# A two-layer decoder trunk: the shared expert's gate and up products moved ahead of the first routed expert, in four PSUM banks

## The chip, the cores and the metric

The kernel runs on one core of one Trainium2 chip. The metric is the device time in microseconds of one execution. A core has a matrix engine (TensorE, PE in the rows), VectorE (DVE), ScalarE (ACT), GpSimd (POOL) and SyncE (SP), which here does nothing but issue transfers. Its 16 DMA engines bring data from HBM into the on-chip SBUF; matrix products land in PSUM, which has eight banks of 128 x 512 float32.

## What is computed

Two decoder layers run over 272 tokens (16 learned ones and 256 of input) of width 1024. Layer 0 mixes tokens with RWKV-7, layer 1 with sliding-window attention. After each mixer stands a mixture of 64 small SwiGLU experts with 8 chosen per token, and one shared expert for all tokens:

```
def swiglu(x, wg, wu, wd):
    return (jax.nn.silu(x @ wg) * (x @ wu)) @ wd

def moe_ffn(x2d, router, bias, w_gate, w_up, w_down, sh_gate, sh_up, sh_down):
    scores = jax.nn.sigmoid(x2d.astype(F32) @ router.astype(F32))
    ...                                   # 4 of 8 groups, then 8 of 64 experts per token
    y = lax.map(expert_block, ...)        # swiglu(x2d[tok], w_gate[e], w_up[e], w_down[e]) * gate
    routed = jax.ops.segment_sum(y.reshape(P, D), slot_tok, num_segments=T)
    return swiglu(x2d, sh_gate, sh_up, sh_down) + routed
```

All is float32. An expert's three matrices (1024 x 256, 1024 x 256 and 256 x 1024) are 1 MiB each, so the 64 experts of a layer are 192 MiB that must be read from HBM.

## The kernel before

Every engine has its program written out by hand, and counting semaphores join them. `Steps` gives each named step of a stage a place in a list, and a later engine waits for "step x is done".

**The expert stage.** Experts are worked off in order, one turn each. In turn e TensorE does the gate and up products of expert e (`mm_gate_up`, L782), turns the gathered token rows of expert e+1 (`mm_turn_x`, L770), picks the token indices of expert e+3 (`pe_pick`, L763: three columns wide), turns the hidden values (`mm_turn`, L789) and does the down product of expert e-1 (`mm_down`, L800). VectorE makes the index lists (`dve_mark`, L807, and `dve_index`, L813 to L815) and copies the turned rows (L775); GpSimd gathers token rows by an indirect DMA (L819) and scatters results (L824).

**Weights.** There are 18 slots of 1 MiB in SBUF, six experts' worth: `ORDER` names them by threes (gate, up, down). SyncE issues the loads, strictly in order. The loads of experts 0 to 4 (15 slots) are issued before the stage. Slots 15, 16 and 17, which belong to expert 5, lie in memory that the router and the shared expert use first: slot 15 holds the shared gate weights, slot 16 the shared up weights, slot 17 part of what the shared products read (`mhT` lies in it in part). `plan_experts` says what frees them. From expert 6 on, the gate and up loads of expert e wait for the gate and up products of expert e-6, and its down load for the down product of expert e-6 (`sp_load`):

```
for slot in (15, 16, 17):
    slot_free[slot] = moe_pe[l].at("su1")
```

**The shared expert.** `mm_shared` makes one of four products: gate and up, each in two halves of the hidden width (`sg0`, `sg1`, `su0`, `su1`), in eight steps over the model width, each step two instructions of 128 x 272 in the trace (L1014). Gate halves both go to bank 7 and up halves both to bank 1, so `sg1` waits until ScalarE has taken `sg0`, and `su1` until VectorE has taken `su0`. `sg0` and `su0` run while VectorE ranks the experts; `sg1` and the first half of `su1` come after the picks of experts 0 to 2; the second half of `su1` is in turn 0, behind `mm_turn`. The six down products (`mm_shared_down`, L1024) are in turns 1, 2 and 3, two in each. `keep_busy` (L1005) issues matrix products whose result nobody reads.

Of the kernel before, what the change touches and what calls it, by code (L numbers as in the profile page):

```python
# [123 lines left out]
def hybrid_trunk(nc, I, out):  # L124
    with ExitStack() as ctx:
# [127 lines left out]
        def ln_steps(t, halves=True):  # L253
# [25 lines left out]
        H_ORDER = [(0, 2, 1), (1, 2, 0)]  # L279
        ROW_ORDER = [(0, 1, 0, 2, 1), (1, 0, 1, 2, 0)]  # L280
        moe_pe = [Steps(sem(f"route_pe{l}"), [(f"hT{t}", 1 if t == 2 else 2) for t in H_ORDER[l]]
                        + [("lg", 1), ("sT", 1), ("sg0", 1), ("su0", 1), ("pos", 1), ("sg1", 1), ("su1", 1), ("sd", 6)])
                  for l in range(2)]
        moe_act = [Steps(sem(f"route_act{l}"), [(f"hT{t}", 1) for t in H_ORDER[l]] + [("sig", 1), ("sc", 1), ("sg0", 1), ("sg1", 1)]) for l in range(2)]
        moe_dve = [Steps(sem(f"route_dve{l}"),
                         [(f"{n}{t}", 1) for n, t in zip(("hT", "hT", "row", "row", "row"), ROW_ORDER[l])]
                         + [("choice", 1), ("top2", 24), ("gs", 1), ("rank", 5), ("hide", 1), ("mask", 1),
                            ("top8", 3), ("taken", 3), ("sel", 1), ("g0", 1), ("gsum", 1), ("g1", 1), ("g2", 1),
                            ("kr", 1), ("dest", 3), ("posm", 1), ("max", 1), ("maxi", 1), ("sm0", 1), ("sm1", 1),
                            ("sd", 6)]) for l in range(2)]  # L290
        ON_PE, ON_DVE_FIRST, ON_DVE_LAST = (0, 1, 3, 5), (2, 4), (6, 7)
        NORM = ("st0", "st1", "mv", "sub", "rec", "out")
# [139 lines left out]
        def plan_experts(l):  # L432
            if l == 0:
                for slot in range(RING, 15):
                    slot_free[slot] = rv.at(f"y_{NCH - 1}")
            else:
                for slot in range(RING, 12):
                    slot_free[slot] = end_dve[0].end()
                for slot in (12, 13):
                    slot_free[slot] = av.at("add4")  # L440
                slot_free[14] = av.at(f"add{LAST}")
            for slot in (15, 16, 17):
                slot_free[slot] = moe_pe[l].at("su1")
            main_slots.append((list(slot_count), list(slot_free)))
            done = (l + 1) * E
            for i, slot in enumerate(ORDER):
                slot_count[slot] += 16 * len(range(i // 3, E, SETS))
                slot_free[slot] = (main.down if i % 3 == 2 else main.gu, done)
# [264 lines left out]
        bV, bU, bG, bR, bY = 0, 2, 3, 4, (5, 6)  # L713

        bL, bT_, bS, bC = 5, 6, (7, 1), 5

# [7 lines left out]
        def wait(eng, s, value):  # L726

            if not isinstance(value, int) or value > 0:
                eng.wait_ge(s, value)

        def early(e, k):

            return isinstance(e[0], int) and e[1] == k
# [52 lines left out]
        def mm_turn(dst):  # L786

            for j in range(2):
                mm = nc.tensor.transpose(dst[:, P * j:P * j + P], guc[:, P * j:P * j + P], ident[:, :])  # L789
            return mm  # L790
# [72 lines left out]
        def pe_expert(pe, L, l, e, this=True):  # L863
            after, three_after, prev = ahead(e, 1), ahead(e, 3), e_before(e)
            if this:
                s0, s1, _ = e_slots(e)
                pe.wait_ge(L.xt_copied, num(e, 1, L.base + 1))
                pe.wait_ge(slot_loaded[s0], num(e, 16, L.slot_base[s0] + 16, per=SETS))
                pe.wait_ge(slot_loaded[s1], num(e, 16, L.slot_base[s1] + 16, per=SETS))
                wait(pe, L.gu_copied, num(e, 1, L.base))  # L870
                mm_gate_up(ps[:, bG, :], (s0, s1)).then_inc(L.gu, 1)
            if this and after:
                pe_turn_x(pe, L, l, plus(e, 1))
            if this and three_after:
                pe_pick(pe, L, plus(e, 3))
            if this:
                copied, hidden = num(e, 1, L.base + 1), num(e, 1, L.base)
                if not isinstance(copied, int):
                    pe.reg_add(copied_count, copied_count, 1)
                    pe.reg_add(hidden_count, hidden_count, 1)  # L880
                    copied, hidden = copied_count, hidden_count
                pe.wait_ge(*moe_dve[l].at("choice"))
                pe.wait_ge(L.gu_copied, copied)
                wait(pe, L.hid, hidden)
                mm_turn(ps[:, bR, :]).then_inc(L.turned, 1)
            if prev:
                q = plus(e, -1)
                s2 = e_slots(q)[2]
                pe.wait_ge(L.hid, num(q, 1, L.base + 1))
                if early(q, 0):  # L890
                    pe.wait_ge(*moe_dve[l].at("maxi"))
                pe.wait_ge(slot_loaded[s2], num(q, 16, L.slot_base[s2] + 16, per=SETS))
                wait(pe, L.y_a, num(q, 1, L.base - 1))
                wait(pe, L.y_v, num(q, 1, L.base - 1))
                mm_down(ps[:, bY[q[1] % 2], :], s2, hidT[q[1] % 2]).then_inc(L.down, 1)
# [106 lines left out]
        def keep_busy(bank, n):  # L1002

            for _ in range(n):
                nc.tensor.matmul(ps[:, bank, :], ident[:, :], router[:, 0, :, :].rearrange("p k e -> p (k e)"), start=True,  # L1005
                                 stop=True)

        def mm_shared(pe, l, name, ks):

            which, half = name[1], int(name[2])  # L1010
            j = "gu".index(which)
            for k in ks:
                w = shared_w[j][:, FF * k:FF * k + FF].rearrange("p (m j) -> p j m", j=2)
                m = nc.tensor.matmul(ps[:, bS[j], 0:T], w[:, half, :], mhT[:, k, :], start=(k == 0), stop=(k == KC - 1))  # L1014
                if k == KC - 1:
                    m.then_inc(*moe_pe[l].step(name))

# [10 lines left out]
        def pe_experts(pe, L, l):  # L1028
            pe.reg_mov(copied_count, num((0, HEAD - 1), 1, L.base + 1))
            pe.reg_mov(hidden_count, num((0, HEAD - 1), 1, L.base))  # L1030
            keep_busy(SPARE_BANK[1], 1)
            pe_pick(pe, L, (0, 0))
            pe_pick(pe, L, (0, 1))
            pe_pick(pe, L, (0, 2))
            pe.wait_ge(*moe_act[l].at("sg0"))
            mm_shared(pe, l, "sg1", range(KC))
            pe.wait_ge(*moe_dve[l].at("sm0"))
            mm_shared(pe, l, "su1", range(KC // 2))
            pe_turn_x(pe, L, l, (0, 0))

            def body(e):
                pe_expert(pe, L, l, e)
                if early(e, 0):
                    mm_shared(pe, l, "su1", range(KC // 2, KC))
                if early(e, 1):
                    pe.wait_ge(*moe_dve[l].at("sm1"))
                    pe.wait_ge(shared_loaded[2], 16 * (l + 1))
                if isinstance(e[0], int) and 1 <= e[1] <= 3:
                    for u in (2 * e[1] - 2, 2 * e[1] - 1):
                        mm_shared_down(pe, l, u)  # L1050
            over_experts(pe, body)
            pe_expert(pe, L, l, (0, E), this=False)

        def act_silu(act, l, half):
            act.wait_ge(*moe_pe[l].at(f"sg{half}"))
            nc.scalar.activation(shid[:, half, :], ps[:, bS[0], 0:T], ACT.Silu).then_inc(*moe_act[l].step(f"sg{half}"))

        def act_experts(act, L, l):
            act_silu(act, l, 1)
# [3 lines left out]
        def dve_shared(dve, l, half):  # L1063
            dve.wait_ge(*moe_act[l].at(f"sg{half}"))
            dve.wait_ge(*moe_pe[l].at(f"su{half}"))
            nc.vector.tensor_tensor(shm[:, half, :], shid[:, half, :], ps[:, bS[1], 0:T], ALU.mult)\
                .then_inc(*moe_dve[l].step(f"sm{half}"))

        def dve_shared_down(dve, l, u):
# [7 lines left out]
        def dve_experts(dve, L, l):  # L1077
            dve_mark(dve, L, (0, 0))
            dve_mark(dve, L, (0, 1))
            dve_index(dve, L, (0, 0))  # L1080
            dve_mark(dve, L, (0, 2))
            dve_index(dve, L, (0, 1))
            dve_index(dve, L, (0, 2))
            nc.vector.tensor_reduce(most, ps[:, bC, NT * E:NT * E + E], AX.X, ALU.max).then_inc(*moe_dve[l].step("max"))
            dve.wait_ge(*moe_dve[l].at("max"))
            nc.vector.tensor_copy(mosti_of[l], most).then_inc(*moe_dve[l].step("maxi"))
            dve_shared(dve, l, 0)
            dve_copy_xt(dve, L, (0, 0))

            def body(e):  # L1090
                dve_expert(dve, L, e)
                if early(e, 0):
                    dve_shared(dve, l, 1)
                if isinstance(e[0], int) and 1 <= e[1] <= 3:
                    for u in (2 * e[1] - 2, 2 * e[1] - 1):
                        dve_shared_down(dve, l, u)
            over_experts(dve, body)
            dve_expert(dve, L, (0, E), this=False)
# [333 lines left out]
        def _(pe):  # L1432
# [373 lines left out]
            def moe(l, prev_dve):  # L1806
# [24 lines left out]
                nc.tensor.transpose(ps[:, bT_, 0:P], score_T[:, 0:P], ident[:, :])  # L1831
                nc.tensor.transpose(ps[:, bT_, P:P + E], score_T[E:P, P:2 * P], ident[E:P, E:P]).then_inc(*st.step("sT"))
                mm_shared(pe, l, "sg0", range(2, KC))
                pe.wait_ge(shared_loaded[1], 16 * (l + 1))
                mm_shared(pe, l, "su0", range(KC))

                pe.wait_ge(*moe_dve[l].at("sel"))
                for t in range(NT + 1):
# [997 lines left out]
```

## Time and profile before

| | us |
|---|---|
| median of 3 runs | 1638.23 (1637.66 to 1640.96) |
| the profiled execution | 1638.7 |
| its span in the trace | 1637.0 |

The profiled execution took 1638.7 us, of which the trace's span from the first to the last instruction is 1637.0. TensorE was busy 1454.8 us, VectorE 614.0, ScalarE 318.5 and GpSimd 328.2; the mean granted TensorE clock was 0.968 of full speed. The expert stage runs in layer 0 from about 382 to 889 us and in layer 1 from about 1089 to the last scatter near the end.

How to read the rows: a row of the timeline gives the start, the duration, engine, line, operation, result and sources, the number of instructions merged into it, and in brackets how long the engine was idle before it and what released it. SPq is SyncE's queue: its rows are issues of transfers, so their duration is that of the issue and not of the transfer.

### The profile page before, as it was taken

How to read it: one execution, taken by the hardware profiler on the slowest of the kernel's cores; microseconds unless marked ns; L12 is line 12 of the kernel's file. 1: busy time of each engine (PE TensorE's matmuls, PEld its weight loads, DVE VectorE, ACT ScalarE, POOL GpSimd, SP SyncE). 2: the span in 40 equal slices, each digit the busy share in tenths (PEclk: the TensorE clock that was granted, in tenths of full speed). 3: DMA queues.
4: the chain of work that ended last, by engine and by line, in shares of the span. 5: the costliest groups of instructions: out<-in, count | busy, mean ns of one | idle time of the engine just before them, and what ended most of it. 6: DMA issues, size and time to landing. Idle time of an engine off the chain costs nothing.

```text
span 1637.0 us, 33339 instructions
## 1 busy us (share of the span) xinstructions
PE 1454.8 (89%) x12808; PEld 943.1 (58%) x12808; DVE 614.0 (38%) x1580; ACT 318.5 (19%) x743; POOL 328.2 (20%) x404
## 2 busy tenths in 40 slices
PE   6989988899999988888886698999999888888884
PEld 4776877656566655555553267565666555555541
DVE  5362352673333333223321704543333333333326
ACT  1621333110111111111111015111111111111110
POOL 6012000011232222222222120112322222222210
PEclk9999988899999999999999899999999999999997
DMA  7330002685999999999997995439999999999986
GB/s 201 125 116 1 4 4 80 221 324 198 414 412 412 415 416 415 415 415 415 415 415 292 370 294 206 146 126 415 413 414 414 416 414 415 415 415 416 414 346 251
DMA packets 139878, 508.42 MB, mean 311 GB/s; under 512 B 29273, under 2 KB 58273, under 8 KB 104188
## 3 DMA queue, kind: packets, MB, share of 16 engines
q1 hardware_dynamic: 103312, 456.49, 70.0%
q0 software_dynamic: 22288, 41.89, 7.1%
q10 hardware_dynamic: 14172, 8.54, 1.9%
q8 instruction: 77, 1.26, 0.3%
q14 instruction: 29, 0.24, 0.0%
HBM read 501.38 MB, written 36.90 MB: 329 GB/s over the span
## 4 chain that ended last, share of the span: by engine, by line
PE 46%; SPq 33%; DMA 8%; DVE 6%; issue 3%; ACTq 3%; ACT 1%; POOL 0%; POOLq 0%; DVEq 0%
SPq L834 33%; PE ps L782 10%; DMA arena<-in_moe_w_up 6%; PE ps L1466 6%; PE ps L800 5%; PE ps L1596 3%; ACTq L2225 3%; PE ps L763 2%; PE ps L1014 2%; PE ps L2001 2%; PE ps L770 2%; PE ps L1024 1%; DMA arena<-routed 1%; DVE h L2705 1%; PE ps L789 1%
## 5 line engine op out<-in xcount | busy, mean ns | idle before, releaser
L782 PE MATMUL ps<-arena 128*64 128x256 f32 x2752 | 316.2, 382 | 61.2 <-DMA arena<-in_moe_w_up 49.5
L782 PEld LDWEIGHTS ps<-arena 128*64 128x64 f32 x2752 | 214.2, 137 | 193.6 <-issue 126.5
L775 DVE COPY arena<-ps 128x512 f32<-128x512 f32 x128 | 88.5, 692 | 471.7 <-PE ps L770 471.7
L819 POOL DMA_INDIRECT arena<-hrows,arena x128 | 130.4, 1019 | 568.1 <-DVE arena L815 555.1
L782 PE MATMUL ps<-ring,arena 128*64 128x256 f32 x1344 | 153.5, 381 | 26.1 <-DMA ring<-in_moe_w_up 24.5
L824 POOL DMA_INDIRECT routed<-arena x128 | 117.3, 917 | 246.0 <-DVE arena L948 226.9
L800 PE MATMUL ps<-arena 128*64 128x512 f32 x688 | 166.6, 605 | 0.0
L948 DVE TENSOR_SCALAR arena<-ps,arena 64x512 f32<-64x512 f32 x128 | 95.1, 743 | 167.7 <-PE ps L800 167.7
L782 PEld LDWEIGHTS ps<-ring,arena 128*64 128x64 f32 x1344 | 99.8, 137 | 93.8 <-issue 36.4
L902 ACT COPY arena<-ps 128x256 f32<-128x256 f32 x128 | 47.7, 373 | 488.2 <-PE ps L782 488.2
L912 ACT ACTIVATE arena<-ps,arena 64x512 f32<-64x512 f32 x128 | 87.6, 684 | 208.2 <-PE ps L800 208.2
L763 PEld LDWEIGHTS ps<-arena 128*128 128x128 f32 (+1 forms) x768 | 105.6, 190 | 6.1 <-issue 2.3
L763 PE MATMUL ps<-arena 128*128 (+3 forms) x768 | 105.8, 242 | 2.1 <-DVE arena L815 2.1
L770 PE MATMUL ps<-ident,arena 128*128 128x128 f32 x512 | 83.8, 286 | 0.0
L770 PEld LDWEIGHTS ps<-ident,arena 128*128 128x128 f32 x512 | 53.8, 141 | 48.7 <-issue 48.5
L800 PE MATMUL ps<-ring,arena 128*64 128x512 f32 x336 | 81.3, 604 | 0.0
L800 PEld LDWEIGHTS ps<-arena 128*64 128x64 f32 x688 | 41.8, 136 | 63.5 <-issue 63.5
L1466 PE MATMUL ps<-arena,ring 128*128 128x272 f32 x256 | 64.2, 416 | 8.3 <-DVE arena L2379 4.4
L807 DVE SCALAR_TENSOR_TENSOR arena<-arena 128x384 f32<-128x384 f32 x128 | 69.2, 542 | 0.1
L906 ACT ACTIVATE arena<-ps 128x128 f32<-128x128 f32 x128 | 35.5, 278 | 152.4 <-PE ps L789 152.4
L1466 PEld LDWEIGHTS ps<-arena,ring 128*128 128x128 f32 x256 | 51.9, 203 | 20.4 <-DVE arena L2379 4.5
L789 PE MATMUL ps<-ident,arena 128*128 128x128 f32 x256 | 55.8, 299 | 1.0 <-issue 1.0
(360 smaller groups left out, 1532.8 us busy)
## 6 DMA issues: line engine op xcount, KB each, us to landing
arena<-in_moe_w_down SPq DMA_DIRECT2D x86, 1024.0 KB, 24.2
arena<-in_moe_w_gate SPq DMA_DIRECT2D x86, 1024.0 KB, 24.7
arena<-in_moe_w_up SPq DMA_DIRECT2D x86, 1024.0 KB, 24.8
ring<-in_moe_w_gate SPq DMA_DIRECT2D x42, 1024.0 KB, 24.6
ring<-in_moe_w_up SPq DMA_DIRECT2D x42, 1024.0 KB, 24.5
ring<-in_moe_w_down SPq DMA_DIRECT2D x42, 1024.0 KB, 24.3
arena<-routed SPq DMA_DIRECT2D x16, 1024.0 KB, 14.7
ring<-in_attn_w_qkv SPq DMA_DIRECT2D x6, 1024.0 KB, 16.4
```

The costliest lines, as they stand in the source:

```text
L763: mm = nc.tensor.matmul(dst[:, 0:3], hot[0:n, t, :], vals[0:n, t, :], start=(t == 0), stop=(t == NT - 1))
L770: mm = nc.tensor.transpose(dst[:, P * j:P * j + P], rows[:, P * j:P * j + P], ident[:, :])
L775: return nc.vector.tensor_copy(xgT.rearrange("p (r j) m -> p j r m", r=2), ps[:, bU, :].rearrange("p (j r m) -> p j r m", j=4, r=2))
L782: mm = nc.tensor.matmul(dst[SLOTS * j:SLOTS * j + SLOTS, 0:FF], xgT[:, k, :], slots[pair[j]][:, FF * k:FF * k + FF], start=(k == 0), stop= ...
L789: mm = nc.tensor.transpose(dst[:, P * j:P * j + P], guc[:, P * j:P * j + P], ident[:, :])
L800: mm = nc.tensor.matmul(dst[SLOTS * half:SLOTS * half + SLOTS, :], hid[:, j, :], slots[s][:, D * j + 512 * half:D * j + 512 * half + 512], ...
L819: return nc.gpsimd.indirect_dma_start(out=dst, out_offset=None, in_=hrows_d[l], in_offset=bass.IndirectOffsetOnAxis(ap=index, axis=0), bou ...
L824: return nc.gpsimd.indirect_dma_start(out=routed[l], out_offset=bass.IndirectOffsetOnAxis(ap=index, axis=0), in_=src, in_offset=None, boun ...
L834: sp.dma_start(slot_view(s, j), expert_weights(l, num(e))[j]).then_inc(slot_loaded[s], 16)
L912: nc.scalar.activation(ysc[q[1] % 2][:, 512:1024], ps[SLOTS:P, bY[q[1] % 2], :], ACT.Copy, scale=gate_s[q[1] % INDICES][SLOTS:P]).then_inc ...
L948: nc.vector.tensor_scalar(ysc[q[1] % 2][:, 0:512], ps[0:SLOTS, bY[q[1] % 2], :], gate_s[q[1] % INDICES][0:SLOTS], None, ALU.mult).then_inc ...
L1466: m = mm_(b[:, 0:T], slot3(s)[:, k, P * (c % 2):P * (c % 2) + P], xm[MIXBUF[mix]][:, k, :], start=(k == 0), stop=(k == KC - 1))
```

## The change

The four shared halves get a bank each (7, 3 for gate, 1, 4 for up). `sg1` takes the place of `su0` while VectorE ranks. `su0` and `su1` run whole between the three picks, in the place of `keep_busy` and of the old `sg1` and first half of `su1`; turn 0 loses its part of `su1`. Slot 15 is free after `sg1` instead of `su1`. Banks 3 and 4 are those of `mm_gate_up` and `mm_turn`, so TensorE waits for ScalarE's `sg1` before it turns the rows of expert 0, and for VectorE's `sm1` before `mm_turn` of turn 0. On VectorE `sm0` comes ahead of the third index, the copy of expert 0's rows ahead of the two small steps `max` and `maxi`, and `sm1` ahead of turn 0.

```
-                        + [("lg", 1), ("sT", 1), ("sg0", 1), ("su0", 1), ("pos", 1), ("sg1", 1), ("su1", 1), ("sd", 6)])
+                        + [("lg", 1), ("sT", 1), ("sg0", 1), ("sg1", 1), ("pos", 1), ("su0", 1), ("su1", 1), ("sd", 6)])
...
-            for slot in (15, 16, 17):
+            slot_free[15] = moe_pe[l].at("sg1")
+            for slot in (16, 17):
                 slot_free[slot] = moe_pe[l].at("su1")
...
+        bH = ((7, 3), (1, 4))
...
+                if early(e, 0):
+                    pe.wait_ge(*moe_dve[l].at("sm1"))
                 mm_turn(ps[:, bR, :]).then_inc(L.turned, 1)
...
-                m = nc.tensor.matmul(ps[:, bS[j], 0:T], w[:, half, :], mhT[:, k, :], start=(k == 0), stop=(k == KC - 1))
+                m = nc.tensor.matmul(ps[:, bH[j][half], 0:T], w[:, half, :], mhT[:, k, :], start=(k == 0), stop=(k == KC - 1))
...
-            keep_busy(SPARE_BANK[1], 1)
+            pe.wait_ge(shared_loaded[1], 16 * (l + 1))
+            mm_shared(pe, l, "su0", range(2))
             pe_pick(pe, L, (0, 0))
+            mm_shared(pe, l, "su0", range(2, KC))
             pe_pick(pe, L, (0, 1))
+            mm_shared(pe, l, "su1", range(KC // 2))
             pe_pick(pe, L, (0, 2))
-            pe.wait_ge(*moe_act[l].at("sg0"))
-            mm_shared(pe, l, "sg1", range(KC))
-            pe.wait_ge(*moe_dve[l].at("sm0"))
-            mm_shared(pe, l, "su1", range(KC // 2))
+            mm_shared(pe, l, "su1", range(KC // 2, KC))
+            pe.wait_ge(*moe_act[l].at("sg1"))
             pe_turn_x(pe, L, l, (0, 0))
 
             def body(e):
                 pe_expert(pe, L, l, e)
-                if early(e, 0):
-                    mm_shared(pe, l, "su1", range(KC // 2, KC))
                 if early(e, 1):
-                    pe.wait_ge(*moe_dve[l].at("sm1"))
                     pe.wait_ge(shared_loaded[2], 16 * (l + 1))
...
             dve_index(dve, L, (0, 1))
+            dve_shared(dve, l, 0)
             dve_index(dve, L, (0, 2))
+            dve_copy_xt(dve, L, (0, 0))
             nc.vector.tensor_reduce(most, ps[:, bC, NT * E:NT * E + E], AX.X, ALU.max).then_inc(*moe_dve[l].step("max"))
...
-            dve_shared(dve, l, 0)
-            dve_copy_xt(dve, L, (0, 0))
+            dve_shared(dve, l, 1)
...
                 mm_shared(pe, l, "sg0", range(2, KC))
-                pe.wait_ge(shared_loaded[1], 16 * (l + 1))
-                mm_shared(pe, l, "su0", range(KC))
+                mm_shared(pe, l, "sg1", range(KC))
```

Here is TensorE's program in layer 0 from the end of the position counts to the turning of expert 0's rows, before the change. L1005 is `keep_busy`, L763 a pick, L1014 the shared expert, L770 the turning; here the order counts one row item for one product of the program.

```order
L1005 MATMUL ps<-router,ident 128x512
L763 MATMUL ps<-arena 128x3 [waits onehot_made]
L763 MATMUL ps<-arena 128x3 x2
L763 MATMUL ps<-arena 128x3 [waits index_ready,onehot_made]
L763 MATMUL ps<-arena 128x3 x2
L763 MATMUL ps<-arena 128x3 [waits index_ready,onehot_made]
L763 MATMUL ps<-arena 128x3 x2
L1014 MATMUL ps<-arena 128x272 [waits route_act0]
L1014 MATMUL ps<-arena 128x272 x7
L1014 MATMUL ps<-arena 128x272 [waits route_dve0]
L1014 MATMUL ps<-arena 128x272 x3
L770 MATMUL ps<-ident,arena 128x128 [waits gathered0]
```

The twelve shared products stand in one block behind the picks, eight of `sg1` and four of `su1`. The same place after the change, where the lines are L1018 (shared), L765 (pick) and L772 (turning):

```order
L1018 MATMUL ps<-arena 128x272 [waits shared_loaded1]
L1018 MATMUL ps<-arena 128x272
L765 MATMUL ps<-arena 128x3 [waits onehot_made]
L765 MATMUL ps<-arena 128x3 x2
L1018 MATMUL ps<-arena 128x272 x6
L765 MATMUL ps<-arena 128x3 [waits index_ready,onehot_made]
L765 MATMUL ps<-arena 128x3 x2
L1018 MATMUL ps<-arena 128x272 x4
L765 MATMUL ps<-arena 128x3 [waits index_ready,onehot_made]
L765 MATMUL ps<-arena 128x3 x2
L1018 MATMUL ps<-arena 128x272 x4
L772 MATMUL ps<-ident,arena 128x128 [waits gathered0,route_act0]
```

Now there are sixteen shared products, eight of `su0` and eight of `su1`, spread between the picks. Next is TensorE at the end of turn 0 in layer 0, before the change, from the turning of the hidden values (L789) to the gate and up products of expert 1 (L782) and what follows them.

```order
L789 MATMUL ps<-ident,arena 128x128 [waits gate_up_copied,route_dve0]
L789 MATMUL ps<-ident,arena 128x128
L1014 MATMUL ps<-arena 128x272 x4
L782 MATMUL ps<-arena 64x256 [waits slot_loaded8,gate_up_copied,slot_loaded7,xt_copied]
L782 MATMUL ps<-arena 64x256 x15
```

And the same place after the change (L791 and L784):

```order
L791 MATMUL ps<-ident,arena 128x128 [waits route_dve0,gate_up_copied]
L791 MATMUL ps<-ident,arena 128x128
L784 MATMUL ps<-arena 64x256 [waits slot_loaded8,gate_up_copied,slot_loaded7,xt_copied]
L784 MATMUL ps<-arena 64x256 x15
L772 MATMUL ps<-ident,arena 128x128 [waits xt_copied,gathered2]
```

The four shared products between the two are gone.

## Rows read from the trace of the kernel before

**Rows 1.** The page's first line: the span.
```profile
span 1637.0 us, 33339 instructions
```

**Rows 2.** Busy time, granted clock, DMA share and GB/s by stretch, two stretches.
```profile
core 0: us, PE busy (x) PEld busy (x) DVE busy (x) ACT busy (x) POOL busy (x), PEclk, DMA share, GB/s
...
385.00:390.00 5.00, 5.00 (x36) 3.70 (x34) 1.56 (x6) 0.65 (x2) 1.00 (x1) 1.00 0.01 3
600.00:700.00 100.00, 86.28 (x633) 53.55 (x630) 29.90 (x84) 16.02 (x36) 23.74 (x25) 1.00 1.02 415
```

**Rows 3.** Waits of all engines: us in total, times, longest.
```profile
PE ps L782 <- DMA arena<-in_moe_w_up: 49.5, 39, 2.4
...
PE ps L782 <- DMA ring<-in_moe_w_up: 24.5, 23, 1.5
```

**Rows 4.** Waits of SyncE's queue, same columns.
```profile
SPq L834 <- PE ps L1014: 81.8, 2, 41.8
```

**Rows 5.** Timeline of SyncE's queue, layer 0: issues of gate weights.
```profile
389.64 0.33 SPq L834 DMA_DIRECT2D arena<-in_moe_w_gate  x1
...
414.82 0.33 SPq L834 DMA_DIRECT2D arena<-in_moe_w_gate  x1
...
425.45 0.33 SPq L834 DMA_DIRECT2D ring<-in_moe_w_gate  x1
...
432.37 0.33 SPq L834 DMA_DIRECT2D arena<-in_moe_w_gate  x1
...
576.81 6.74 SPq L834 DMA_DIRECT2D ring<-in_moe_w_gate  x1
...
841.59 6.89 SPq L834 DMA_DIRECT2D arena<-in_moe_w_gate  x1
```

**Rows 6.** Issue to landing of the gate loads issued at 389.64, 425.45 and 1131.73.
```profile
DMA to landing us min/median/max: 4.8/4.8/4.8
...
DMA to landing us min/median/max: 7.6/7.6/7.6
...
DMA to landing us min/median/max: 8.2/8.2/8.2
```

**Rows 7.** Timeline of TensorE, layer 0, picks to turn 1.
```profile
370.18 0.92 PE L763 MATMUL ps<-arena 128*128 128x3 f32 x6
...
373.85 7.42 PE L1014 MATMUL ps<-arena 128*128 128x272 f32 x24
381.11 0.60 PE L770 MATMUL ps<-ident,arena 128*128 128x128 f32 x4
...
386.59 0.81 PE L763 MATMUL ps<-arena 128*128 128x3 f32 x6
387.33 0.44 PE L789 MATMUL ps<-ident,arena 128*128 128x128 f32 x2
387.61 2.01 PE L1014 MATMUL ps<-arena 128*128 128x272 f32 x8
389.54 3.67 PE L782 MATMUL ps<-arena 128*64 128x256 f32 x32
```

**Rows 8.** Timeline of TensorE, layer 1, the same place.
```profile
1075.23 0.92 PE L763 MATMUL ps<-arena 128*128 128x3 f32 x6
...
1087.39 0.60 PE L770 MATMUL ps<-ident,arena 128*128 128x128 f32 x4
...
1095.83 3.67 PE L782 MATMUL ps<-arena 128*64 128x256 f32 x32
```

**Rows 9.** Stretches of 1 us, columns as in group 2.
```profile
372.00:373.00 1.00, 0.51 (x4) 0.41 (x4) 0.34 (x3) 0.00 (x0) 0.56 (x1) 1.00 0.00 0
...
375.00:376.00 1.00, 1.00 (x4) 0.77 (x3) 0.00 (x0) 0.00 (x0) 0.74 (x1) 0.50 0.35 70
...
1081.00:1082.00 1.00, 1.00 (x4) 0.77 (x3) 0.01 (x1) 0.00 (x0) 0.85 (x1) 0.50 0.46 135
```

**Rows 10.** Issue to landing of all 128 gathers, L819.
```profile
DMA to landing us min/median/max: 2.9/6.7/10.6
```

More of the change, by code:

```diff
@@ L288, in hybrid_trunk @@
                             ("top8", 3), ("taken", 3), ("sel", 1), ("g0", 1), ("gsum", 1), ("g1", 1), ("g2", 1),
-                            ("kr", 1), ("dest", 3), ("posm", 1), ("max", 1), ("maxi", 1), ("sm0", 1), ("sm1", 1),
+                            ("kr", 1), ("dest", 3), ("posm", 1), ("sm0", 1), ("max", 1), ("maxi", 1), ("sm1", 1),
                             ("sd", 6)]) for l in range(2)]
@@ L1055, in act_silu @@
             act.wait_ge(*moe_pe[l].at(f"sg{half}"))
-            nc.scalar.activation(shid[:, half, :], ps[:, bS[0], 0:T], ACT.Silu).then_inc(*moe_act[l].step(f"sg{half}"))
+            nc.scalar.activation(shid[:, half, :], ps[:, bH[0][half], 0:T], ACT.Silu).then_inc(*moe_act[l].step(f"sg{half}"))
         def act_experts(act, L, l):
@@ L1065, in dve_shared @@
             dve.wait_ge(*moe_pe[l].at(f"su{half}"))
-            nc.vector.tensor_tensor(shm[:, half, :], shid[:, half, :], ps[:, bS[1], 0:T], ALU.mult)\
+            nc.vector.tensor_tensor(shm[:, half, :], shid[:, half, :], ps[:, bH[1][half], 0:T], ALU.mult)\
                 .then_inc(*moe_dve[l].step(f"sm{half}"))
@@ L1086, in dve_experts @@
             nc.vector.tensor_copy(mosti_of[l], most).then_inc(*moe_dve[l].step("maxi"))
-            dve_shared(dve, l, 0)
-            dve_copy_xt(dve, L, (0, 0))
+            dve_shared(dve, l, 1)
             def body(e):
                 dve_expert(dve, L, e)
-                if early(e, 0):
-                    dve_shared(dve, l, 1)
                 if isinstance(e[0], int) and 1 <= e[1] <= 3:
```

## The prediction

> **What bounds the kernel now.** The span is 1637.0 us [rows 1]; the profiled execution took 1638.7 and the median is 1638.23, so a sum made in the trace carries over to the median as it is.
>
> I began with the waits, since TensorE's high busy share says nothing about what ends last. In the expert stages TensorE stands at the gate and up products (L782) and waits for weight transfers, 49.5 + 24.5 = 74.0 us in 62 waits over both layers [rows 3]. The stretches say the same from the other side: from 600 to 700 us the DMA share is 1.02 at 415 GB/s, with TensorE 86% busy [rows 2]. SyncE's queue gives the pace. Early in the stage gate loads follow each other by what TensorE needs for a turn, 432.37 - 425.45 = 6.92 us; later, from 576.81 to 841.59, 32 turns take 264.78 us, 8.27 each [rows 5]. So a turn costs TensorE 6.92 us and the transfers 8.27. After a dozen turns the weights set the end of the stage, and stay the bound: it ends when the last expert's weights have landed, plus one fixed turn.
>
> Then the question is when the transfers lose time. The row for 385 to 390 us shows a DMA share of 0.01 [rows 2]: transfers that bound the stage stand still. SyncE's waits say why: it stood 81.8 us in two waits (one a layer) for the shared product at L1014 [rows 4]. It resumes at 389.64 [rows 5], when the last part of `su1` in turn 0 is done and frees slots 15 to 17; TensorE begins turn 1's products at 389.54 [rows 7].
>
> **How much idle time can be had back.** Not all. Starting earlier helps only until the transfers run out of free slots, since those of expert e wait for TensorE's turn e-6. Turns 1 to 3 are long, because each has two shared down products: the loads of experts 9 and 10 are issued 425.45 - 414.82 = 10.63 us apart [rows 5], while three transfers take 8.27. So a queue that starts with a lead loses some 2.4 us of it in each long turn, and the tightest point is the last of them, the gate load of expert 10 at 425.45, released by turn 4's gate and up products. After it turns take 6.92 against 8.27, and the backlog grows again.
>
> At this point before, the load took 7.6 us from issue to landing. The load of expert 5 at 389.64, which met an empty queue, took 4.8 [rows 6]. So 7.6 - 4.8 = 2.8 us of backlog stood ahead of it. In layer 1 the same load took 8.2 [rows 6], a backlog of 8.2 - 4.8 = 3.4. If the queue gets there empty, the gain of a layer is this backlog plus whatever earlier time TensorE finishes turn 4's gate and up products. An empty queue costs the 4.8 us there, which is in the sum.
>
> The Trainium skill ("DMA: Bandwidth & Descriptors", section on the anatomy of one DMA) gives about 2.0 us fixed plus size over 436 GB/s, 4.4 us for 1 MiB, where the row has 4.8. By it the backlog would be 0.4 more in each layer and the gain 0.8 us more; the row decides.
>
> **The change on TensorE.**
> 1. `sg1` for `su0` while VectorE ranks: same eight steps, nothing.
> 2. The first two steps of `su0` replace `keep_busy`. Eight instructions of a shared product cost 389.54 - 387.61 = 1.93 us from start to start at full clock [rows 7], so these four cost 0.97. The first pick starts at 370.18 as before [rows 7]: it waits for VectorE's first index list, which doesn't move.
> 3. From there three picks, at 387.33 - 386.59 = 0.74 us each [rows 7], make 2.22; the twelve instructions left of `su0` 2.90; `su1` 2 x 1.93 = 3.86. Together 8.98, so expert 0's rows are turned at 379.16 instead of 381.11: 1.95 us earlier. Sixteen shared steps stand here where twelve stood, two of them ahead of the first pick, and yet the stretch gets shorter, for two reasons. The waits between picks, where TensorE idled while VectorE made an index, are filled; and the half clock goes: the granted clock was 0.50 in 375 to 376 us, just after 372 to 373 in which TensorE was 0.51 busy [rows 9]. The 24 instructions at 373.85 took 381.11 - 373.85 = 7.26 us, against 3 x 1.93 = 5.79 at full clock [rows 7], a loss of 1.5.
> 4. In layer 1 the same stretch ran from 1075.23 to 1087.39 [rows 8], 12.16 us, since the half clock was there too [rows 9] and lasted longer. 12.16 - 8.98 = 3.18 us earlier.
> 5. Turn 0 loses four steps of `su1`: 1.93 us in each layer. TensorE then needs expert 1's turned rows at once; VectorE's copy of them ends at about the time that `mm_turn` does, so I price that at nothing, at most 0.2.
>
> TensorE reaches turn 1, and with it turn 4, 1.95 + 1.93 = 3.9 us earlier in layer 0 and 3.18 + 1.93 = 5.1 in layer 1.
>
> **Does the queue get there empty?** Slot 15 is loaded while nothing else is. Slots 16 and 17 start at 379.2. That is 10.5 us earlier than 389.64, plus one transfer (8.27 / 3 = 2.76): a lead of 13.2 us, against 6.7 that can be used (2.8 + 3.9). In layer 1 the queue resumed with turn 1's products at 1095.83 [rows 8]; less 1075.23 + 8.98 = 1084.2 that is 11.6, plus 2.76 makes 14.4 against 8.5. So it does, in both.
>
> **Edits priced at nothing.** `sm0` ahead of the third index on VectorE waits for `su0`, which ends before the second pick, so VectorE has it while TensorE makes `su1`. The third gather then comes some 3 us later, at about 378.7; a gather takes 2.9 to 10.6 us to land [rows 10], so at the worst it is there at 389.3, when TensorE turns those rows in turn 1, at about 389.3. That is cover without a margin at its worst, and 4 us at the median of 6.7. The second gather, issued near 376, is wanted near 384. `sm1` ahead of `mm_turn` of turn 0 is ready at about 381.5, before TensorE can ask at 385. The wait for `sg1` on ScalarE is over ten microseconds earlier. If one of these covers fails, what is late next is turn 1 or 2, and so the release at 425.45, microsecond for microsecond.
>
> **The sum.** Layer 0: 2.8 + 3.9 = 6.7. Layer 1: 3.4 + 5.1 = 8.5. Together 15.2 us, and 1638.2 - 15.2 = 1623.0.
>
> **The rivals.**
> - *Half clock stays.* The spells of half clock between the picks and expert 0 come again. They cost 1.5 us in layer 0 (step 3) and 1.5 + 12.16 - (381.11 - 370.18) = 2.7 in layer 1. Gain 15.2 - 4.2 = 11.0: 1627.2. For it: the picks stay narrow, and `keep_busy` goes. Against: the idle half microseconds that stood ahead of the drop are filled with wide products. The Trainium skill ("TensorE: Matmul & The Clock Gate", Part 1) says the throttled clock is the default and activity lifts it, so filling the gaps should keep it up; the row with 0.51 busy ahead of the drop agrees in kind.
> - *Only TensorE's shift counts.* If 7.6 and 8.2 us are what a load takes at this point even in an empty queue, with gathers and scatters between, there is no backlog to win: 3.9 + 5.1 = 9.0, 1629.2. Against it: the next gate loads take longer again, as a growing queue would.
> - *The whole lead counts.* 13.2 + 14.4 = 27.6 us, 1610.6. It needs the long turns not to drain the lead; the issues 10.63 us apart [rows 5] speak against it.
> - *The stage isn't bound by transfers at its end,* so a start moved by a few us is swallowed: 1638. The 74.0 us of waits speak against.
> - *Slower.* With `keep_busy` gone, TensorE falls to half clock in the first turns. It decides for the worse only when TensorE reaches turn 4 later than before by more than the backlog, so when it has lost 6.7 us in layer 0 and 8.5 in layer 1. Half clock through turns 0 and 1, some 18 us of work at full clock, would lose 18 us a layer: 36 - 15.2 = 20.8 slower, 1659. Turn 0 ran at full clock behind a gap like that before, so little speaks for it.
>
> **How the numbers follow.** Forecast 72 in 100, its own range 1619 to 1626 (0.8 us a layer for the landing of 4.8 under other traffic and for step 5). Half clock stays, in one or both layers, 11; only TensorE's shift 7; the whole lead 4; no change 3; slower 3. What a measurement of this kernel can tell from no change is 0.2%, 3.3 us. The range takes in the second and third case: 1617 to 1630. Faster by over 0.2% is 72 + 11 + 7 + 4 = 94, within it 3, slower 3.
>
> **What the changed profile would show.** SyncE issues slot 15's gate load near 366.6 and the next near 379.2 in layer 0, a gap where the DMA share is zero. Expert 0's rows are turned near 379.2 and 1084.2, expert 1's products start near 385.7 and 1090.7. The granted clock is 1.00 between. Gate loads of experts 8 to 10 land about 5 us after issue and that of expert 10 is issued near 421.6; from there each load stands some 6.7 us earlier than before, to the end of the stage, with TensorE's waits for weights a few us longer in sum than 74. The prediction is wrong if the granted clock falls in turns 0 to 3, if expert 10's load still takes over 7 us to land, or if a turn among the first three waits for a gather.

## The result, and the profile after

In the comparison of the two kernels, ten executions of each, the median is 1635.03 us (1629.94 to 1641.89) after the change and 1641.28 us (1637.31 to 1650.9) before. The ratio is 0.9951, with a 95% interval of 0.9933 to 0.9969: by the ratio 8 us less (the two medians are 6.3 apart), where 15.2 were forecast, and 1635.0 lies above the range of 1617 to 1630. A second set of the same kernel (below) gave 0.9922 [0.9894, 0.9949].

The profiled execution after the change took 1635.15 us. Its page begins:

```profile
span 1633.4 us, 33331 instructions
```

That is only 3.6 us less than 1637.0 [rows 1], less than the ratio says. To see why, the trace must be cut. The stage of a layer is measured here from its first shared product (L1014 before, L1018 after) to the start of its last down product (L800, L802). These are the rows of TensorE's timeline before the change:

```profile
358.50 1.19 PE L1014 MATMUL ps<-arena 128*128 128x272 f32 x4
...
887.11 1.89 PE L800 MATMUL ps<-ring,arena 128*64 128x512 f32 x8
...
1063.55 1.19 PE L1014 MATMUL ps<-arena 128*128 128x272 f32 x4
...
1593.37 1.89 PE L800 MATMUL ps<-ring,arena 128*64 128x512 f32 x8
```

and after it:

```profile
366.63 1.19 PE L1018 MATMUL ps<-arena 128*128 128x272 f32 x4
...
890.61 1.89 PE L802 MATMUL ps<-ring,arena 128*64 128x512 f32 x8
...
1066.91 1.19 PE L1018 MATMUL ps<-arena 128*128 128x272 f32 x4
...
1590.44 1.89 PE L802 MATMUL ps<-ring,arena 128*64 128x512 f32 x8
```

The stage of layer 0 went from 528.61 to 523.98 us (-4.63), that of layer 1 from 529.82 to 523.53 (-6.29), together -10.9. The part ahead of layer 0's stage, which the change does not touch, was 8.13 us longer in this execution (366.63 against 358.50); it hides most of the gain in this one trace. Between the stages -0.1, behind them -0.7. Both of these findings want an explanation: 10.9 in the stages instead of 15.2, and the 8.13 ahead of them.

The 8.13 first. These are the stretches ahead of layer 0's stage, before and after the change (columns as in [rows 2]):

```profile
0.00:358.50 358.50, 318.04 (x5105) 249.28 (x5106) 166.69 (x348) 100.29 (x221) 52.10 (x111) 0.93 0.35 118
...
0.00:366.63 366.63, 326.39 (x5105) 254.08 (x5105) 167.10 (x348) 100.76 (x221) 52.03 (x111) 0.91 0.34 115
```

TensorE ran the same 5105 instructions in both. Its mean granted clock was 0.93 before and 0.91 after, and it was busy 8.35 us longer, while the busy times of VectorE, ScalarE and GpSimd differ by less than 0.5 us. So this part was longer because TensorE's clock was lower in that execution. The change has no part in that, as run 1 shows below.

TensorE in layer 0, the picks (L765) and the shared products (L1018) to turn 1, in the timeline after the change:

```profile
378.31 0.92 PE L765 MATMUL ps<-arena 128*128 128x3 f32 x6
379.16 3.02 PE L1018 MATMUL ps<-arena 128*128 128x272 f32 x12
382.02 0.81 PE L765 MATMUL ps<-arena 128*128 128x3 f32 x6
382.76 2.11 PE L1018 MATMUL ps<-arena 128*128 128x272 f32 x8
384.71 0.81 PE L765 MATMUL ps<-arena 128*128 128x3 f32 x6
385.45 2.11 PE L1018 MATMUL ps<-arena 128*128 128x272 f32 x8
387.40 0.60 PE L772 MATMUL ps<-ident,arena 128*128 128x128 f32 x4
...
393.99 3.67 PE L784 MATMUL ps<-arena 128*64 128x256 f32 x32
```

No idle time stands between the rows, and the eight instructions of half a product take 384.71 - 382.76 = 1.95 us. From the first shared product to turn 1's products it is 393.99 - 366.63 = 27.36 us, against 389.54 [rows 7] - 358.50 = 31.04 before: 3.68 earlier. In layer 1 it is again 27.36, against 1095.83 [rows 8] - 1063.55 = 32.28: 4.92 earlier.

SyncE's queue in layer 0 after the change, gate loads only (columns as before: start and duration of the issue):

```profile
374.79 0.33 SPq L836 DMA_DIRECT2D arena<-in_moe_w_gate  x1
...
419.27 0.33 SPq L836 DMA_DIRECT2D arena<-in_moe_w_gate  x1
...
429.91 0.34 SPq L836 DMA_DIRECT2D ring<-in_moe_w_gate  x1
...
436.82 0.34 SPq L836 DMA_DIRECT2D arena<-in_moe_w_gate  x1
...
443.74 0.33 SPq L836 DMA_DIRECT2D ring<-in_moe_w_gate  x1
```

The first is slot 15's, 8.2 us after the stage began; the load of expert 10, at 429.91, is 63.28 us after it, against 425.45 [rows 5] - 358.50 = 66.95 before. The waits of the queue and of TensorE:

```profile
SPq L836 <- PE ps L784: 113.8, 32, 6.7
...
SPq L836 <- PE ps L1018: 59.5, 4, 17.5
```

```profile
PE ps L784 <- DMA arena<-in_moe_w_up: 45.8, 36, 2.4
...
PE ps L784 <- DMA ring<-in_moe_w_up: 26.7, 24, 1.5
```

The two waits of 81.8 us for a shared product [rows 4] have become four of 59.5, the longest 17.5 instead of 41.8. TensorE still waits 72.5 us for weights (74.0 before [rows 3]): the stages still end by the transfers.

**Where the transfers stand.** The stretches of 90 us from each stage's first shared product, before the change (the last columns are the granted clock, the DMA share and GB/s):

```profile
358.50:448.50 90.00, 88.17 (x540) 55.09 (x540) 35.75 (x129) 11.99 (x27) 17.09 (x21) 0.98 0.73 289
...
1063.55:1153.55 90.00, 88.17 (x533) 55.75 (x532) 35.07 (x125) 11.72 (x26) 17.14 (x21) 0.96 0.71 283
```

and after it, with the stretch around the release of expert 10's slots:

```profile
366.63:456.63 90.00, 89.22 (x568) 55.96 (x568) 36.85 (x131) 12.66 (x28) 19.15 (x24) 1.00 0.82 310
...
429.00:432.00 3.00, 3.00 (x24) 1.92 (x22) 1.28 (x5) 0.65 (x2) 0.00 (x0) 1.00 0.54 143
...
1066.91:1156.91 90.00, 89.22 (x568) 55.96 (x568) 36.86 (x131) 12.66 (x28) 19.21 (x24) 1.00 0.82 312
```

This is the reading that shows where the size comes from. At the end of each stretch the queue is full in both kernels and moves 412 to 415 GB/s from then on (415 in [rows 2]). So what the stage gains is what more the transfers have moved by then, over the rate: (310 - 289) x 90 / 415 = 4.6 us in layer 0 and (312 - 283) x 90 / 415 = 6.3 in layer 1. The stages got 4.63 and 6.29 shorter. The same sum, made with the stretches of the other eight traces, gives what each of their sixteen stages gained or lost within 0.4 us.

### The profile page after: what moved, and what is told of

Its sections match the earlier page's. It is cut to its first block, busy times and chain, and to the rows that moved or that the text cites. A ratio compares the mean times of both kernels' runs of the same rounds, so it can differ in the third digit from the quotient of the medians.

```text
span 1633.4 us, 33331 instructions
## 1 busy us (share of the span) xinstructions
PE 1457.5 (89%) x12804; PEld 944.0 (58%) x12804; DVE 614.2 (38%) x1580; ACT 318.8 (20%) x743; POOL 327.6 (20%) x404
## 4 chain that ended last, share of the span: by engine, by line
PE 50%; SPq 32%; DMA 8%; DVE 5%; issue 3%; ACT 1%; POOL 0%; POOLq 0%; DVEq 0%; ACTq 0%
SPq L836 32%; PE ps L784 11%; PE ps L1467 6%; PE ps L802 5%; DMA arena<-in_moe_w_up 5%; PE ps L1597 3%; PE ps L765 2%; PE ps L1018 2%; PE ps L1899 2%; PE ps L772 2%; PE ps L2001 2%; DMA ring<-in_moe_w_up 2%; PE ps L1028 1%; DMA arena<-routed 1%; PE ps L791 1%
## 5 line engine op out<-in xcount | busy, mean ns | idle before, releaser
L784 PE MATMUL ps<-arena 128*64 128x256 f32 x2752 | 316.0, 382 | 57.2 <-DMA arena<-in_moe_w_up 45.8
L784 PEld LDWEIGHTS ps<-arena 128*64 128x64 f32 x2752 | 213.3, 137 | 189.3 <-issue 119.4
L784 PE MATMUL ps<-ring,arena 128*64 128x256 f32 x1344 | 153.6, 381 | 28.3 <-DMA ring<-in_moe_w_up 26.7
L802 PE MATMUL ps<-arena 128*64 128x512 f32 x688 | 166.6, 605 | 0.0
L784 PEld LDWEIGHTS ps<-ring,arena 128*64 128x64 f32 x1344 | 100.1, 137 | 96.0 <-issue 38.6
L765 PEld LDWEIGHTS ps<-arena 128*128 128x128 f32 (+1 forms) x768 | 105.0, 188 | 3.1 <-DVE arena L809 0.7
L765 PE MATMUL ps<-arena 128*128 (+3 forms) x768 | 104.6, 241 | 0.0
L772 PE MATMUL ps<-ident,arena 128*128 128x128 f32 x512 | 83.8, 286 | 0.0
L772 PEld LDWEIGHTS ps<-ident,arena 128*128 128x128 f32 x512 | 53.8, 141 | 48.7 <-issue 48.5
L802 PE MATMUL ps<-ring,arena 128*64 128x512 f32 x336 | 81.3, 604 | 0.0
L802 PEld LDWEIGHTS ps<-arena 128*64 128x64 f32 x688 | 41.8, 136 | 63.5 <-issue 63.5
L791 PE MATMUL ps<-ident,arena 128*128 128x128 f32 x256 | 55.8, 299 | 1.0 <-issue 1.0
```

Of the source, the lines that this page charges most:

```text
L765: mm = nc.tensor.matmul(dst[:, 0:3], hot[0:n, t, :], vals[0:n, t, :], start=(t == 0), stop=(t == NT - 1))
L772: mm = nc.tensor.transpose(dst[:, P * j:P * j + P], rows[:, P * j:P * j + P], ident[:, :])
L784: mm = nc.tensor.matmul(dst[SLOTS * j:SLOTS * j + SLOTS, 0:FF], xgT[:, k, :], slots[pair[j]][:, FF * k:FF * k + FF], start=(k == 0), stop= ...
L802: mm = nc.tensor.matmul(dst[SLOTS * half:SLOTS * half + SLOTS, :], hid[:, j, :], slots[s][:, D * j + 512 * half:D * j + 512 * half + 512], ...
```

## The experiments

Each is compared with the kernel before by timed executions of both on the same chip, and read from its own trace. "Turn 1" is the time from the first shared product to the gate and up products of expert 1, "stage" as above, both for layer 0 / layer 1, and "begins" is where layer 0's stage starts.

| kernel | begins | turn 1 | stage | median | ratio to before |
|---|---|---|---|---|---|
| before | 358.5 | 31.04 / 32.28 | 528.6 / 529.8 | 1641.3 | 1 |
| changed | 366.6 | 27.36 / 27.36 | 524.0 / 523.5 | 1635.0 | 0.9951 [0.9933, 0.9969] |
| 1 changed, again | 359.0 | 29.03 / 27.36 | 525.6 / 523.9 | 1631.6 | 0.9922 [0.9894, 0.9949] |
| 2 slots late | 361.3 | 28.99 / 27.36 | 530.0 / 528.8 | 1640.6 | 0.9978 [0.9953, 1.0004] |
| 3 turn 0 filled up | 364.5 | 33.37 / 33.37 | 529.9 / 529.6 | 1641.8 | 0.9972 [0.9950, 0.9995] |
| 4 down products in turns 1 to 6 | 363.9 | 27.36 / 27.35 | 520.7 / 520.7 | 1624.8 | 0.9861 [0.9831, 0.9890] |
| 5 the same on the kernel before | 361.2 | 31.02 / 32.28 | 528.3 / 529.7 | 1642.3 | 0.9989 [0.9961, 1.0016] |
| 6 slot 15 freed at `su1` | 361.3 | 27.35 / 27.36 | 523.9 / 523.5 | 1631.8 | 0.9939 [0.9907, 0.9971] |
| 7 down products in turns 2 to 7 | 364.0 | 28.99 / 27.35 | 519.8 / 518.3 | 1619.3 | 0.9844 [0.9809, 0.9879] |
| 8 before, again | 364.1 | 32.00 / 31.05 | 529.5 / 528.8 | 1642.0 | 0.9997 [0.9966, 1.0028] |

Runs 1 to 4 shared one set of the kernel before (median 1644.65), runs 5 to 8 another, on a second chip (1643.07).

**1. The changed kernel again.** No edit.

> The changed kernel unaltered, once more. The stage of a layer is measured from the first shared product to the start of the last down product: 528.6 and 529.8 us before, 524.0 and 523.5 in the first trace of the changed kernel. Theory A (the change is worth 4.6 + 6.3 us in the two stages, and the 8.1 us by which the part ahead of layer 0's stage was longer in that trace are scatter of a part that the change does not touch): the stages are again within 0.5 us of 524.0 and 523.5, the start of layer 0's stage lies elsewhere by several us (358 to 367), and the ratio lies near 1 - 11/1640 = 0.993. Rival B (the part ahead is longer by 8 us in the changed kernel each time): the stage starts at 366 to 367 us again and the ratio stays at 0.995 to 0.997.

Rival B is out: the stage began at 359.0 us, as in the first trace of the kernel before, and the kernel before itself began it at 364.1 in its second trace (run 8). The part ahead lies between 358.5 and 366.6 us over ten traces of eight kernels that all run the same program there. Most of that is TensorE's busy time there, which lies between 317.9 and 326.4 us in the ten; the rest of the part, in which it was not busy, lies between 39.5 and 43.0. The ratio came out at 0.992. But layer 0's stage was 525.6, outside the 0.5 us that I gave it. Half clock had come back at the picks, as these stretches of that run show:

```profile
370.00:371.00 1.00, 1.00 (x7) 0.62 (x6) 0.97 (x3) 0.00 (x0) 0.00 (x0) 1.00 0.99 418
371.00:372.00 1.00, 1.00 (x6) 0.96 (x6) 0.46 (x5) 0.00 (x0) 0.00 (x0) 0.74 0.24 98
372.00:373.00 1.00, 1.00 (x3) 0.67 (x2) 0.41 (x1) 0.00 (x0) 0.10 (x1) 0.50 0.00 0
...
374.00:375.00 1.00, 1.00 (x4) 0.77 (x3) 0.00 (x0) 0.00 (x0) 0.09 (x1) 0.55 0.23 43
```

TensorE had no idle time between the picks here either. The clock fell about when the first pick ended, which began at 370.65 us: it is 0.74 in 371 to 372 and 0.50 in 372 to 373. Turn 1 starts 29.03 - 27.36 = 1.67 us later. The stage is longer by the same 1.7.

**2. Slots freed late.** TensorE's order is that of the changed kernel; slots 15 to 17 wait for expert 1's gate and up products.

```
-            slot_free[15] = moe_pe[l].at("sg1")
-            for slot in (16, 17):
-                slot_free[slot] = moe_pe[l].at("su1")
+            for slot in (15, 16, 17):
+                slot_free[slot] = (main.gu, l * E + 2)
```

> The changed kernel, but slots 15 to 17 are free only after expert 1's gate and up products (TensorE's order as in the changed kernel). The transfers then resume 31.0 us after the first shared product, as before the change (31.1), while TensorE stays 3.7 and 4.9 us earlier. Theory A (transfers set the end of the stage): both stages are back at 528.5 +- 1 us, so the ratio is 0.999 to 1.001. Rival (TensorE's shift counts by itself): stages near 525, ratio near 0.995.

Layer 1, with full clock at the picks, is the clean case: TensorE is 4.9 us earlier than in the first trace of the kernel before, but the transfers resume 31.1 us into the stage against 32.4 there, 1.3 earlier, and the stage is 1.0 us shorter. In layer 0 half clock came again (turn 1 at 28.99), the transfers resumed at 393.98 or 32.7 us into the stage, 1.6 later than before the change, and the stage was 530.0, 1.4 longer and outside the 528.5 +- 1 that I gave it. The ratio of 0.9978 [0.9953, 1.0004] takes in no change and leaves out the rival's 0.995. So theory A holds: the stage follows the time at which the transfers resume, and a shorter way to turn 1 is worth nothing by itself.

**3. Turn 0 filled up.** Seven products that nobody reads, at the end of turn 0, hold TensorE back; the slots are freed early.

```
                 pe_expert(pe, L, l, e)
+                if early(e, 0):
+                    keep_busy(SPARE_BANK[0], 7)
                 if early(e, 1):
```

> The changed kernel, with seven reader-less products (about 3.9 us) at the end of turn 0. TensorE reaches turn 1 within about 0.3 us of its place before the change in layer 0, and 1.0 us earlier in layer 1, while slots 15 to 17 are freed early. What is left of the gain is the backlog term alone. By the prediction it is 2.8 and 3.4 us (read from the gate load of expert 10); by what the changed kernel's trace shows from expert 12 on it is about 1.0 and 1.4. So: stage of layer 0 at 528.6 - 2.8 = 525.8 by the prediction's term, or near 527.8 by the smaller one; layer 1 at 529.8 - 1.0 - 3.4 = 525.4, or near 527.4.

I had sized the filling wrongly. TensorE's timeline of this run:

```profile
391.80 6.17 PE L1009 MATMUL ps<-router,ident 128*128 128x512 f32 x14
397.91 3.67 PE L784 MATMUL ps<-arena 128*64 128x256 f32 x32
```

Fourteen instructions held TensorE for 6.1 us, not 3.9, so turn 1 came at 33.37 in both layers, 2.33 and 1.09 us later than before the change. Layer 1's stage ends with this row:

```profile
1601.07 1.89 PE L802 MATMUL ps<-ring,arena 128*64 128x512 f32 x8
```

It took 1601.07 - 1071.44 = 529.63 us. With the delay counted, the early transfers alone were worth 528.61 + 2.33 - 529.85 = 1.1 us in layer 0, and 529.82 + 1.09 - 529.63 = 1.3 in layer 1. Both are the smaller size (1.0 and 1.4), not the 2.8 and 3.4 of the prediction.

**4. Shared down products one per turn, in turns 1 to 6.** The same edit on TensorE and on VectorE:

```
-                if isinstance(e[0], int) and 1 <= e[1] <= 3:
-                    for u in (2 * e[1] - 2, 2 * e[1] - 1):
+                if isinstance(e[0], int) and 1 <= e[1] <= 6:
+                    for u in (e[1] - 1,):
```

> The changed kernel, with the six shared down products one per turn in turns 1 to 6 instead of two per turn in turns 1 to 3. A turn then costs TensorE 8.8 us instead of 10.6, near the transfers' 8.3. Theory A with slots: TensorE reaches turn 4 some 5.4 us earlier, turn 5 3.6 and turn 6 1.8, so the queue keeps more of its lead and the stages get shorter by another 2 to 4 us each (near 521), ratio near 0.990. Rival (the lead is already used up by something else, the transfers' own rate or gathers among them): the stages stay at 524.0 and 523.5.

Each stage became another 3 us shorter, 520.7. By the 90 us from its first shared product,

```profile
363.93:453.93 90.00, 89.22 (x558) 54.83 (x558) 36.88 (x131) 12.68 (x28) 18.29 (x23) 1.00 0.86 325
```

the transfers had moved (325 - 289) x 90 / 415 = 7.8 us' worth more than before the change, and the stage was 8.0 us shorter. The rival, that the lead had been used up by something else, is out: it was used up by the long turns. The ratio of 0.9861 lies below the 0.990 that I expected. It means 22.9 us, and the two stages make up 17.1 of them; the rest lies outside the stages, and this one trace doesn't explain it.

**5. The same edit on the kernel before.**

> The kernel before, with only the shared down products spread over turns 1 to 6, one each. Theory A (what counts is the idle time of the transfers; before the change they never run empty after turn 1's start, so the long turns cost nothing): stages stay at 528.6 and 529.8 us within 0.7, ratio 0.998 to 1.001, although the same edit on the changed kernel made its stages 520.7. Rival (shorter early turns are a gain of their own): stages 3 us shorter each, ratio near 0.996.

528.3 and 529.7: nothing, as expected. The long turns cost nothing there, because the queue never ran empty behind turn 1: in this run's layer 0 the gate loads of experts 7 to 13 took 11 to 16 us to land. They became a cost only with the change.

**6. Slot 15 freed with the others.**

```
-            slot_free[15] = moe_pe[l].at("sg1")
-            for slot in (16, 17):
+            for slot in (15, 16, 17):
                 slot_free[slot] = moe_pe[l].at("su1")
```

> The changed kernel, but slot 15 is freed with slots 16 and 17, after su1, as in the kernel before. The first transfer then comes 12.8 us later. Theory A (the queue runs empty at experts 9 and 10 in any case, so a larger lead is thrown away): stages stay at 524.0 and 523.5 within 0.5 us. Rival (every transfer moved forward counts): each stage longer by one transfer, 2.5 to 2.8 us.

523.9 and 523.5, within 0.1 us those of the changed kernel. Of the change's parts, the early freeing of slot 15 brought nothing: that megabyte arrives early into a queue that empties anyway (expert 10's gate load took 4.9 us to land here too). What `sg1` ahead of `su0`, and the bank for it, are worth by themselves no run shows.

**7. Shared down products in turns 2 to 7.** As in run 4, with `2 <= e[1] <= 7` and `u = e[1] - 2`.

> The changed kernel with the six shared down products one per turn in turns 2 to 7. TensorE releases the slots of experts 8 to 13 one product (1.8 us) earlier than with turns 1 to 6 and expert 14's at the same time. With turns 1 to 6 the gate loads up to expert 13 took 5.2 to 6.1 us to land, so the queue was near empty up to there; expert 14's took 10.8. Theory A: the stages get shorter by 0.5 to 1.8 us more (519 to 520), ratio 0.985. Rival (nothing left to win, the lead is already used up): 520.7 as with turns 1 to 6.

519.8 with half clock at the picks in layer 0 (turn 1 at 28.99), 518.3 without it in layer 1, 2.4 less than in run 4; I had expected at most 1.8. Its ratio of 0.9844 [0.9809, 0.9879] is the lowest of the study: 25.6 us less than before, of which the two stages make up about 20. Its interval and that of run 4 overlap. A kernel with the change and this edit has the shortest stages measured here.

**8. The kernel before again.** No edit.

> The kernel before, unaltered, as a second trace of it. Stages 528.6 and 529.8 if the half clock falls at the picks again, up to 1.5 us (layer 0) and 2.7 us (layer 1) shorter if it does not; 497.5 us from the start of expert 1's gate and up products to the last down product in either case. The start of layer 0's stage may lie anywhere from 358 to 367 us. Ratio 1.000 within its interval.

The ratio is 0.9997. Half clock fell at the picks in both layers again. Layer 1's stage ends with

```profile
1600.08 1.89 PE L800 MATMUL ps<-ring,arena 128*64 128x512 f32 x8
```

and took 1600.08 - 1071.33 = 528.75 us. From turn 1 on the stages took 497.5 and 497.7 us, as in the first trace. The twelve executions of this run also show how time and clock go together: the longest, 1660.11 us, had a mean granted clock of 0.955, the shortest, 1636.91, one of 0.968.

## Why the prediction was wrong

The mechanism was right, and the size of one term was not. Point by point:

- *What bounds the kernel.* Right. Transfers set the end of the stage (runs 2 and 5), and the gain is the idle time taken from them, in both layers to the rounding of the GB/s. TensorE's waits for weights went from 74.0 to 72.5 us, though, where "a few us longer" was forecast.
- *TensorE's shift, 3.9 and 5.1 us.* 3.68 and 4.92 in the first trace. The sixteen shared steps and three picks took 387.40 - 378.31 = 9.09 us, where 8.98 were forecast.
- *"Does the queue get there empty?"* Right, nearly. The load of expert 10 landed as fast as one into an empty queue; its landing row after the change, followed by those of the next loads (up of 10, down of 9, gate of 11, gate of 12), is

```profile
DMA to landing us min/median/max: 4.7/4.7/4.7
...
DMA to landing us min/median/max: 7.9/7.9/7.9
...
DMA to landing us min/median/max: 8.3/8.3/8.3
...
DMA to landing us min/median/max: 7.3/7.3/7.3
...
DMA to landing us min/median/max: 9.8/9.8/9.8
```

- *"So 7.6 - 4.8 = 2.8 us of backlog stood ahead of it"*, and 3.4 in layer 1. This is the step that failed. For that one load it is exact: it landed 429.91 + 4.7 - 366.63 = 68.0 us into the stage, against 425.45 + 7.6 - 358.50 = 74.55, 6.6 us earlier, where 6.7 were forecast. But the gain did not last. Before the change the up load of expert 10, the gate load of 11 and that of 12 took

```profile
DMA to landing us min/median/max: 9.7/9.7/9.7
...
DMA to landing us min/median/max: 9.2/9.2/9.2
...
DMA to landing us min/median/max: 10.7/10.7/10.7
```

so they came only 1.8, 1.9 and 0.9 us sooner behind their issue. By the load of expert 12, the queue's part of the gain was 0.9 us, and the stage kept 4.63 - 3.68 = 0.95 in layer 0 and 6.29 - 4.92 = 1.37 in layer 1. A single load into an empty queue does not measure what stands in a full one. The prediction says that an empty queue costs the 4.8 us of that load, "which is in the sum"; but the sum has them for this one load only, and in a part of that time little is moved at all. Around the release of expert 10's slots the transfers fell to 143 GB/s in layer 0 (429 to 432 us, above) and to 130 in layer 1, where before the change they went on. These are the stretches at the same place, layer 0 before, layer 1 before, layer 1 after:

```profile
424.50:427.50 3.00, 3.00 (x24) 1.97 (x22) 1.28 (x5) 0.65 (x2) 0.00 (x0) 1.00 1.01 412
...
1130.80:1133.80 3.00, 3.00 (x24) 1.96 (x22) 1.28 (x5) 0.65 (x2) 0.00 (x0) 1.00 1.00 412
...
1129.27:1132.27 3.00, 3.00 (x24) 1.93 (x22) 1.28 (x5) 0.65 (x2) 0.00 (x0) 1.00 0.52 130
```

What was not moved there was owed later. An estimate from these rows is (412 - 143) x 3 / 415 = 1.9 us' worth in layer 0 and (412 - 130) x 3 / 415 = 2.0 in layer 1 (the edges of the stretches are mine, so a few tenths are open). Taken from 2.8 and 3.4, that leaves 0.9 and 1.4, about what the stages kept. Run 3 gives the same size by an experiment, 1.1 and 1.3. That the gathers and scatters of the turn, which a full queue had interleaved, are part of what was owed is an argument only; no run separates them. The prediction's other figure for a lone load, 4.4 us from the Trainium skill ("DMA: Bandwidth & Descriptors", section "Anatomy of one DMA"), is given there for transfers that GpSimd issues, and these loads are SyncE's; the sum did not use it.
- *The signs.* The prediction named three signs of being wrong: a falling clock in turns 0 to 3, over 7 us for expert 10's load, a wait for a gather in the first turns. In the first trace of the changed kernel none of them came, and the forecast failed all the same: they look at the first turns and at one load, and the gain was lost with the loads behind it.
- *The sum.* With the terms as measured, 3.68 + 0.95 + 4.92 + 1.37 = 10.9 us instead of 15.2. The rival "only TensorE's shift counts" had 9.0 and is the nearest in kind: the shift makes up 8.6 of the 10.9. "Half clock stays" had 11.0, nearly the measured figure, but by luck: in the trace that gave 10.9 the half clock at the picks was gone.
- *"Half clock stays"* had 11 in 100. It stays in part. At the picks it showed in all six stages of the old order (turn 1 at 31.0 to 32.3), and in three of fourteen of the new order (runs 1, 2 and 7, layer 0), at 1.6 to 1.7 us each. With the idle gaps filled it came more rarely, and still came. Whether the filled gaps or the other order of the products did that, no run separates.
- *The rest.* 1641.3 - 10.9 = 1630.4; the measured 1635.0 is higher by more than the half clock explains. Over the first set the ratio means 8 us (5 to 11), over run 1's 12.8 (8.4 to 17.4), over run 6's, whose stages are those of the changed kernel, 10.0 (4.8 to 15.3). The stages' own difference in the mean, 10.2 us between the two traces of the kernel before (the first and run 8) and the three of the new order in runs 1 and 6 and the first, lies in all three. I took the 1638.2 of three executions as the level to start from; later sets of the same kernel have medians of 1641.3 to 1644.7. So the miss of the absolute time, 1635.0 - 1623.0 = 12.0 us, is 3.1 of starting level, 4.3 of the backlog and TensorE's shift, and 4.6 that no trace accounts for; the interval of the ratio, 5 to 11 us, is wider than that.

What stays open is why the granted clock, and with it the part ahead, varies so much from one execution to the next, and why half clock comes at the picks in some stages only.

## What to carry to other kernels

Where transfers bound a loop, a lead given to them at its start is kept only if they never run out of free slots behind it: here 13 us of lead became 4.6 us in layer 0, of which 3.7 are TensorE's earlier release of the slots and only 1 the lead's own, and the next edit, which evened out the long turns that had cost nothing so far, brought another 3 us in each stage, and 4 to 5 with turns 2 to 7. To size such a gain, do not take it from the landing time of one transfer; count the bytes moved in a stretch that starts at the same step and ends where the queue is full in both kernels, and divide by the full rate. And when a kernel's unchanged part varies by more than the gain, measure the stage in the trace from step to step; ten executions gave the ratio to 0.2 or 0.3%, and one trace's span gave a third of the gain.

## What the runs showed of the hardware

- The granted clock fell to 0.50 at the picks of run 1 although TensorE had no idle time in the stretch, only products three columns wide next to ones of 64 and 272 columns; in eleven of fourteen stages with the same program at the picks it did not.
- With the same 5105 TensorE instructions, the part ahead of layer 0's stage took 358.5 us at a mean granted clock of 0.93 and 366.6 at 0.91.
- Transfers restarted by a release fell to 143 GB/s over 3 us around it, against 412 at the same place with the queue full, although the queue had been handed work again 2 us before that stretch ended.
